# An encoder layer with a mixture of experts: first-expert rows written with the residual, GpSimd's loop placed anew, the routing tail reordered

## The reference

```python
h = x + token_mixer(rms_norm(x, g_attn_norm), ...)       # attention and pooling heads, then w_out
a = rms_norm(h, g_ffn_norm)
gp = softmax(a @ w_group_router + b_group_router)         # 4 groups, the best one is taken
el = a @ w_expert_router + b_expert_router                # 32 experts, 8 in a group
e_val, e_idx = top_k(softmax(el of the chosen group), 2)  # two experts of that group per token
y = 0
for e in range(32):
    hdn = silu(a @ w_gate[e]) * (a @ w_up[e])             # 1024 -> 256
    y = y + combine[:, e:e+1] * (hdn @ w_down[e])         # 256 -> 1024
return h + y
```

## Time and profile before

| | |
|---|---|
| median of 3 runs | 606.67 us |
| the profiled execution | 608.44 us |
| its span, first to last instruction | 606.7 us |
| granted TensorE clock, mean | 0.967 |
| TensorE busy | 536.3 us (88%) |
| VectorE, ScalarE, GpSimd busy | 218.0, 168.9, 139.8 us |
| bytes moved by DMA | 140.97 MB |
| read from and written to HBM | 131.15 MB and 16.46 MB |
| start of the weight stream | 257 us |
| first matmul of the expert stage | 328 us |

### The profile page before, as it was taken

The page is one execution under the profiler, slowest core; times in us unless marked ns, Lnnn a source line. Parts: engine busy times, 40 slices in busy tenths (PEclk is TensorE's granted clock), DMA queues, the critical chain, the costliest instruction groups (busy, mean ns, idle before and its releaser), DMA issues.

```text
span 606.7 us, 9491 instructions
## 1 busy us (share of the span) xinstructions
PE 536.3 (88%) x3304; PEld 393.1 (65%) x3305; DVE 218.0 (36%) x602; ACT 168.9 (28%) x421; POOL 139.8 (23%) x230
## 2 busy tenths in 40 slices
PE   4899999999989999999978888878987699897794
PEld 4888988987557677788867545555644456554451
DVE  4754234333657755427772112202111112211111
ACT  6743343332434333125431201202111012111010
POOL 0232232222503300004535022222211222222212
PEclk9999999999989999999987999999998979998978
DMA  8741000012312111199979689999999999999993
GB/s 339 269 116 36 19 18 1 19 51 77 111 63 97 42 36 36 35 357 421 398 263 303 223 264 368 361 365 378 360 372 384 411 393 375 375 354 382 372 392 56
DMA packets 33458, 140.97 MB, mean 232 GB/s; under 512 B 10489, under 2 KB 11148, under 8 KB 21351
## 3 DMA queue, kind: packets, MB, share of 16 engines
q1 hardware_dynamic: 25776, 124.33, 53.6%
q0 software_dynamic: 5856, 12.60, 8.7%
q10 hardware_dynamic: 1766, 3.25, 1.4%
HBM read 131.15 MB, written 16.46 MB: 243 GB/s over the span
## 4 chain that ended last, share of the span: by engine, by line
DMA 36%; PE 16%; DVE 2%; issue 2%; ACT 1%; POOL 0%; SPq 0%; ACTq 0%; DVEq 0%; POOLq 0%
DMA expert_w<-in_w_gate 17%; DMA expert_w<-in_w_up 17%; PE ps L884 5%; PE ps L900 2%; DMA token_gates<-gate_rows 2%; PE ps L795 2%; PE ps L521 1%; PE ps L522 1%; PE ps L526 1%; PE ps L780 1%; PE ps L823 1%; PE ps L769 1%; PE ps L912 1%; POOL out L1708 0%; PE ps L871 0%
## 5 line engine op out<-in xcount | busy, mean ns | idle before, releaser
L884 PE MATMUL ps<-expert_w,xT 128*64 128x256 f32 x1120 | 128.5, 387 | 15.2 <-issue 5.6
L884 PEld LDWEIGHTS ps<-expert_w,xT 128*64 128x64 f32 x1120 | 93.7, 140 | 53.4 <-issue 23.5
L900 PE MATMUL ps<-expert_w,hT 128*64 128x512 f32 x272 | 66.6, 633 | 17.2 <-DVE hT L1546 16.0
L1702 POOL DMA_INDIRECT out<-y_sb,idx_now x17 | 27.2, 1597 | 161.2 <-issue 85.2
L1539 DVE SCALAR_TENSOR_TENSOR hid<-s_act,gate,ps 128x256 f32<-128x256 f32 x18 | 12.0, 665 | 140.1 <-ACT s_act L1171 140.1
L900 PEld LDWEIGHTS ps<-expert_w,hT 128*64 128x64 f32 x272 | 22.5, 145 | 50.7 <-issue 48.5
L1171 ACT ACTIVATE s_act<-ps,gate 128x256 f32<-128x256 f32 x18 | 8.5, 473 | 132.1 <-PE ps L884 132.1
L521 PE MATMUL ps<-w_in_hi,aT_hi 128*128 128x384 f32 (+2 forms) x120 | 43.7, 369 | 0.0
L522 PE MATMUL ps<-w_in_lo,aT_hi 128*128 128x384 f32 (+2 forms) x120 | 40.8, 345 | 0.0
L1551 DVE COPY y_sb<-ps 128x512 f32<-128x512 f32 x18 | 12.4, 692 | 76.3 <-PE ps L900 70.8
L1176 ACT ACTIVATE y_sb<-ps 128x512 f32<-128x512 f32 x18 | 10.7, 597 | 80.0 <-PE ps L900 74.6
(11 more groups left out here) (229 smaller groups left out, 944.1 us busy)
## 6 DMA issues: line engine op xcount, KB each, us to landing
expert_w<-in_w_up SPq DMA_DIRECT2D x32, 1024.0 KB, 10.0
expert_w<-in_w_gate SPq DMA_DIRECT2D x30, 1024.0 KB, 9.3
expert_w<-in_w_down SPq DMA_DIRECT2D x30, 1024.0 KB, 9.6
w_in_raw<-in_w_in SPq DMA_DIRECT2D x8, 608.0 KB, 8.6
w_out_raw<-in_w_out SPq DMA_DIRECT2D x8, 512.0 KB, 4.1
token_rows<-h_sb ACTq DMA_DIRECT2D x6, 512.0 KB
out<-h_sb SPq DMA_DIRECT2D x6, 512.0 KB, 11.3
x_sb<-in_x_prompt SPq DMA_DIRECT2D x4, 512.0 KB, 10.7
```

What stands on the lines that cost most here:

```text
L884: mm = pe.matmul(ps[r, GU_BANK[q.o], g * FH:(g + 1) * FH], xT[:, q.o, k, r], w_gu(j, b, lane, k, g), start=(k == 0), stop=(k == KD - 1))
L900: mm = pe.matmul(ps[r, 4 + half, :], hT[:, q.o, k, r], w_dn(b, lane, k, half), start=(k == 0), stop=(k == 1))
L1702: pool.indirect_dma_start(out=out, out_offset=bass.IndirectOffsetOnAxis(ap=idx, axis=0), in_=y_sb[:, buf, :], in_offset=None, compute_op=A ...
```

## The change

Five things change together.

1. **A token's row in `out` is written once plainly and once by an add.** A flag says for each slot whether its expert is the lower of the token's two, and so comes first in the order of pairs. The flag is computed in `route_weights` (two more VectorE operations a tile), travels through the slot matmuls as a fourth column block (`slot_b` 3 to 4 blocks, two more ScalarE operations a tile), and lands in the third column of `gate_all`. VectorE's `y_rows` computes flag x gathered row of `h` + result for all 1024 columns in one instruction; it takes the place of the two half copies (ScalarE's stays for pair 15 alone). GpSimd's `put_rows` then issues two indirect transfers a pass: one that writes the flagged rows plainly, and one that adds the others. Each skips the other's rows.
2. **What goes with it.** The six `store_h` and the zero rows are gone, and with them the wait for `h_stored`. A `g_rows` buffer is free when `y_rows` has read it, so GpSimd's gather of pair j + 2 waits for `y_dve` in place of `x_tr`. New tables `put_all` and `put_more` hold the two indices of each slot (VectorE, six small operations), and GpSimd's first overflow gather and loop wait for them (`idx_done` 15 in place of 9).
3. **GpSimd's loop** gets `head_slot`, as TensorE's has: its first instruction lies at the head of a block of instructions that is fetched as one.
4. **The routing tail is reordered.** VectorE does `route_experts` of tile 4 ahead of the last half of the residual. TensorE does `more_slots(2)` and `(3)` while it waits for the last tile, `keep_clock` goes from 40 to 12 matmuls, and the transposes of pair 0's rows come ahead of `more_slots(4)` and `(5)`. VectorE's `x_copy` of pair 0 comes ahead of the overflow tables. The last tile of `token_rows` is stored by SyncE, not by ScalarE.
5. **Weight parts are held up.** Of pair 2 only the two gate parts are issued before the first gather has landed; the up parts wait as well as the down parts.

```diff
@@ signals, pe_y_free, run_pairs, y_free
-            pe.wait_ge(main.y_act, j)
             pe.wait_ge(main.y_dve, j)
-            ... head_slot={eng.engine: 0} if eng.engine == nc.tensor.engine else None
+            ... head_slot={eng.engine: 0} if eng.engine in (nc.tensor.engine, nc.gpsimd.engine) else None
-                eng.wait_ge(main.added, 16 * (n - 2))
+                eng.wait_ge(main.added, 32 * (n - 2))
@@ SyncE
             load_pair(sp, 0, 0)
-            store_h(0)
-            load_pair(sp, 1, 1, range(3))
-            store_h(1)
-            load_pair(sp, 1, 1, range(3, 6))
-            for i in range(2, NT - 1):
-                store_h(i)
+            load_pair(sp, 1, 1)
             sp.wait_ge(o_mm, 2 * NT)
-            store_h(NT - 1)
-            load_pair(sp, 2, 2, range(4))
+            sp.wait_ge(h_done, 2 * NT)
+            sp.dma_start(table[T - P:T, :], h_sb[:, NT - 1, :]).then_inc(rows_stored, 16)
+            load_pair(sp, 2, 2, range(2))
             sp.wait_ge(main.gathered[0], 16)
-            load_pair(sp, 2, 2, range(4, 6))
+            load_pair(sp, 2, 2, range(2, 6))
@@ TensorE
-            for i in range(1, last - 1):
-                more_slots(i)
+            more_slots(1)
             pe.wait_ge(h_done, 2 * NT)
             keep_clock(8)
             ranks(last)
+            first_slots()
+            pe.wait_ge(idx_done, 2)
+            more_slots(2)
+            more_slots(3)
             last_slots()
...
-            pe.wait_ge(idx_done, 5)
-            more_slots(last - 1)
-            more_slots(last)
-            keep_clock(40)
-            pe.wait_ge(counts_done, 1)
+            keep_clock(12)
...
             gather_transposes(main, g_rows[:, 0, :], main.gathered[0], 1)
+            pe.wait_ge(idx_done, 5)
+            more_slots(last - 1)
+            more_slots(last)
+            pe.wait_ge(counts_done, 1)
             run_pairs(pe, pair)
@@ ScalarE
-                store_row(i)
+                if i < NT - 1:
+                    store_row(i)
...
-                y_copy(main, j, b)
+                else:
+                    y_copy(j, b)
@@ VectorE
+                dve.tensor_tensor(is_first(i, 0), R[:, 182:183], R[:, 183:184], ALU.is_lt)
+                dve.tensor_tensor(is_first(i, 1), R[:, 183:184], R[:, 182:183], ALU.is_lt)
...
+                if i == NT - 1:
+                    route_experts(i - 1)
                 residual(i, 1)
...
+            def y_rows(q, n, buf, rows, g):
+                dve.wait_ge(q.y_mm, n + 1)
+                y_free(dve, q, n)
+                dve.scalar_tensor_tensor(out=y_sb[:, buf, :]..., in0=rows..., scalar=gate[:, g, 2:3],
+                                         in1=ps[:, 4:6, :], op0=ALU.mult, op1=ALU.add).then_inc(q.y_dve, 1)
@@ GpSimd
             pool.wait_ge(rows_stored, 16 * NT)
-            pool.wait_ge(h_stored, 16 * NT)
-            def add_rows(q, n, buf, idx):
-                pool.indirect_dma_start(out=out, out_offset=bass.IndirectOffsetOnAxis(ap=idx, axis=0),
+            def put_rows(q, buf, g):
+                pool.indirect_dma_start(out=out, out_offset=bass.IndirectOffsetOnAxis(ap=idx_put[:, g, 0:1], axis=0),
+                                        in_=y_sb[:, buf, :], in_offset=None,
+                                        bounds_check=T - 1, oob_is_err=False).then_inc(q.added, 16)
+                pool.indirect_dma_start(out=out, out_offset=bass.IndirectOffsetOnAxis(ap=idx_put[:, g, 1:2], axis=0),
                                         in_=y_sb[:, buf, :], in_offset=None, compute_op=ALU.add,
                                         bounds_check=T - 1, oob_is_err=False).then_inc(q.added, 16)
...
-                        pool.wait_ge(main.x_tr, j)
+                        pool.wait_ge(main.y_dve, j)
...
-            pool.wait_ge(idx_done, 9)
+            pool.wait_ge(idx_done, 15)
             first_more_gather(0)
```

177 lines of the change are left out of this document (96 added, 81 removed).

## The result

The changed kernel takes 614.98 us (median of 4 runs, 612.01 to 619.3) against 605.83 us for the kernel before on the same chip (4 runs): ratio 1.0152, 95% interval 1.0084 to 1.0220. The profiled execution has a span of 614.0 us, 7.3 us more than the 606.7 us of before, and a mean granted clock of 0.957 against 0.967. The forecast was 602.9 us, range 598.5 to 609.0.

What follows compares the result with a forecast made beforehand. Bound: pair 0's start and overflow pass until 361.5 us, then the DMA weight stream, with TensorE 10.4 us to spare. Sum -5.3 + 1.2 + 0.3 = -3.8 us, from 606.7 to 602.9 us; range 598.5 to 609.0.

Steps and rivals of the forecast that it cites:

- The DMA term: Weight-stream stretch after 361.5 us: plain writes in place of adds save 7.0 us, extra transfers cost 1.7; net -5.3 us.
- its last rival: The gather behind an overflow pass: second scatter 1.9 us behind makes TensorE 5.9 us late, under its 10.4 us slack.
- `y_rows`, +1.2 us: VectorE in pair 0 and its overflow pass: 1.28 us in place of 0.70, twice, delaying the restart by 1.2 us.
- The start, +0.3 us: Routing tail into pair 0: gate matmuls 3.2 us earlier, but the gain spent waiting for overflow rows until 335.6; +0.3 us.
- The rival on the clock: Pair 0 starts at 1.2 GHz after fewer clock-keeping matmuls; if low into the overflow pass, restart 3.5 us later, 606.4 us; chance 0.12.
- its signs of being wrong: q0 as dear as before, pair 4's gate part before 361 or after 366 us, or TensorE waiting only on itself from pair 9.
- The six stores of `h` at 0: Stores removed ahead of the restart: their place in the queue is worth nothing to the stream after 361.5 us; 0.
- the flag's work at 0 to 0.5: Flag operations, fourth slot block and ScalarE copies lie beside TensorE's products on `h` or behind the gather wait: 0, at most +0.5 us.
- The gather behind an overflow pass: After pair 6, doubled transfers delay the next gather; at 7 us per second scatter TensorE is 16.1 us late: 612.4 us; chance 0.11.
- The loop head at 0: GpSimd's loop: GpSimd and its sequencer have 0% of the chain, so placing its code is worth 0.
- The held parts: Pair 2's up parts held back: the first gather meets an idle queue and lands in 4.5 us, at 321.9 us.

Runs made afterwards that it cites:

- run with free gate stores on the old tail: Changed kernel with parts 4 and 5 undone and ScalarE's gate-store wait moved from one tile back to two: 608.88 us, ratio 1.0011 to the kernel before.

## Why the prediction was wrong

- **The DMA term, -5.3 us, held for the stream and failed as kernel time.** It said that q0 would fall from 3.95 to about 3.4 us a MB; it fell to 3.27. The stream took 8.8 us less from pair 4's gate parts to its last parts (221.4 to 212.6 us). But the step that made it kernel time read "whatever takes DMA time out of the loop makes the kernel shorter", and that holds only while the stream is the bound. With TensorE 17.6 us late it wasn't.
- **TensorE's lateness is the term that failed.** By the prediction's own figures (its last rival, with 1.9 us for each second scatter) TensorE would end 10.4 - 5.9 = 4.5 us earlier and the stream 5.3 - 1.5 = 3.8 us earlier: it had 0.7 us to spare. It was 17.6 us late in place of 5.9. The parts are in the points below.
- **`y_rows`, +1.2 us, held.** It takes 1.28 us, as worked out. From the overflow pass's gate matmuls to pair 1 it is 3.7 us longer than before, 2.8 of them the low clock, which leaves 0.8 for it.
- **The start, +0.3 us, failed.** Pair 0 starts at 326.24 (predicted 325.0). The overflow gather goes out at 330.32 (328.8) and takes 6.3 us (6.8), so the rows come at 336.6 and the transposes begin at 337.4, not 335.6. That is 1.8 us of the miss. The larger part was left out: the forecast let TensorE stand for 3.4 us ahead of the overflow pass and charged nothing for its clock behind it. The rival on the clock looked for a clock that stays low from the thinner `keep_clock` on; pair 0's matmuls ran at 2.4 GHz (7.13 us). It fell anew in the wait ahead of the overflow pass, which the prediction had not priced, and cost 2.8 us. Of its signs of being wrong, a gate part of pair 4 after 366 us came true: it went out at 367.98.
- **The six stores of `h` at 0, and the flag's work at 0 to 0.5, failed.** The `h` stage got 3.0 us longer. The prediction looked at what the stores cost the stream, not at what waits for small stores beside it. The run with free gate stores on the old tail shows 0.47% (2.9 us) for it, by the medians 2.1 us, with intervals that overlap by a little; on the new tail none. Why the stores land later with plain writes is open.
- **The gather behind an overflow pass named the right bound, and its number is luck.** It had 0.11 and gave 612.4 us, from 7 us for each second scatter. The second scatters come 1.3 us behind the first, under the 1.9 us at which the same rival called the lateness covered. What was right in it is that TensorE becomes the bound, and its slack of 10.4 us (17.6 - 10.4 = 7.2, against 7.3 in the spans). What it missed is that the slack is shared: 6.5 us of lateness at pair 1, 3.9 us around pair 4 (its weights are waited for longer, and its matmuls take 10.07 in place of 7.13 us), 3.7 us between pairs 5 and 7 (a wait of 1.36 us for the overflow rows and the low clock again), and only then 3.5 us by the chain at pair 9: 17.6 us. The prediction weighed the start and the chain against the slack; the waits at pair 4 and at pair 6's overflow rows, and the clock behind any wait, it did not weigh at all.
- **The loop head at 0 failed.** The reason given was that GpSimd has 0% of the chain before. In the changed kernel GpSimd's issues are on the chain (POOL 1%, and the landings behind them), and in the trace without the placing a stop of 5.53 us falls just there. That it costs kernel time is not clear of the noise. A share of the old chain says nothing of an engine that the change puts on the new one.
- **The held parts**: the run without them shows no difference.

## What to carry to other kernels

Slack against the bound is one account: add up every wait and every delay that a change puts on the second-latest engine, clock loss included, before calling any of them covered. Where a gather is issued behind the landing of a write it doesn't depend on, move it ahead first; only then can a saving in DMA time show, and only as far as the next engine lets it. And a wait for a small store should reach as many tiles back as there are buffers.

## What the runs showed of the hardware

- An indirect transfer that accumulates takes GpSimd 1585 ns to issue, a plain one of the same 128 rows of 4 KB 1020 ns (lines 1725 and 1722 of the changed kernel, 17 of each).
- Three TensorE waits in the expert stage of the changed kernel (4.05, 4.89 and 7.67 us) went with 10.2, 6.8 and 13.6 us at 1.2 GHz, and 64 matmuls of 128x256 then took up to 10.07 us in place of 7.13. Shorter gaps had it too: behind an idle time of 2.64 us ahead of pair 7 they took 8.81 us.
- With half of the scattered rows written plainly, the 16 DMA engines spent 3.27 us a MB on GpSimd's queue in place of 3.98, though each pass has one transfer more.
- Four variants have a stop of 2.73 to 4.88 us inside an unrolled row of matmuls, at the tenth or eleventh of pair 1, with a packet of the instruction queue inside it; it is as large as half the change under study. That it is a wait for code is inferred. A trace of such a kernel should be read for it before its time is believed.
